# A hybrid decoder block in fp32 on one core: the first operands of the output projection prepared under the last merge unit, another order in the feed-forward's first unit, and the residual's reads behind a store

## The reference, cut to what matters

```python
merged = sigmoid(gate_a) * y_a + sigmoid(gate_b) * y_b     # y_a = o @ w_proj_a, y_b = zb @ w_proj_b
h = h + merged @ w_out                                     # 2048 x 2048
hn = rms_norm(h, norm_ffn_w)
h = h + (silu(hn @ w_gate) * (hn @ w_up)) @ w_down         # FFN width 5632
out = rms_norm(h, norm_final_w)[:, 16:]
```

## Time and profile before

| | us |
|---|---|
| median of 3 runs (2781.43 to 2783.2) | 2781.86 |
| the profiled execution | 2782.89 |
| its span, first to last instruction | 2781.1 |
| busy in the span: PE / DVE / ACT / POOL | 2694.5 / 1837.8 / 998.6 / 357.4 |
| mean granted TensorE clock (share of full) | 0.988 |

### The profile page before, as it was taken

How to read it: one execution, slowest core, us unless ns; L and a number is a source line. 1 busy time by engine, 2 the same in 40 slices (tenths; PEclk the granted TensorE clock), 3 DMA queues, 4 the chain that set the end, 5 groups by cost and what they waited for, 6 DMA issues and landing times.

```text
span 2781.1 us, 44509 instructions
## 1 busy us (share of the span) xinstructions
PE 2694.5 (97%) x17640; PEld 2451.1 (88%) x17640; DVE 1837.8 (66%) x1766; ACT 998.6 (36%) x1025; POOL 357.4 (13%) x356
## 2 busy tenths in 40 slices
PE   8999999999999999988979999999999998999997
PEld 7999988888889977867869999999999997788885
DVE  4444555555553234448888888888788887888886
ACT  4433322222222232213344444444444443333333
POOL 5000144444442500110030000000000000000000
PEclk9999999999999999999989999999999999999998
DMA  4333222222223324677434444544445449656661
GB/s 142 91 90 90 77 76 77 82 76 82 75 83 91 106 83 162 233 263 261 138 121 148 143 147 145 171 153 152 148 154 169 147 132 306 232 189 211 214 210 61
DMA packets 345652, 398.70 MB, mean 143 GB/s; under 512 B 11481, under 2 KB 300386, under 8 KB 344418
## 3 DMA queue, kind: packets, MB, share of 16 engines
q1 hardware_dynamic: 286514, 334.34, 37.5%
q10 hardware_dynamic: 59072, 63.44, 6.6%
HBM read 325.92 MB, written 71.83 MB: 143 GB/s over the span
## 4 chain that ended last, share of the span: by engine, by line
PE 92%; DVE 3%; issue 2%; DMA 1%; POOL 1%; ACT 1%; SPq 0%; DVEq 0%; ACTq 0%; POOLq 0%
PE psum L1869 33%; PE psum L2181 10%; PE psum L2180 10%; PE psum L2179 10%; PE psum L2156 6%; PE psum L2157 6%; PE psum L2158 6%; PE psum L2029 2%; PE psum L2024 1%; PE psum L1819 1%; PE psum L1847 1%; DMA w_raw<-in_w_proj_a 1%; PE psum L2008 1%; DVE hq L1657 1%; PE psum L2101 0%
## 5 line engine op out<-in xcount | busy, mean ns | idle before, releaser
L1869 PE MATMUL psum<-hn_lo,w_hi 128*128 128x264 f32 (+1 forms) x1600 | 453.5, 332 | 0.0
L1869 PE MATMUL psum<-hn_hi,w_lo 128*128 128x264 f32 (+1 forms) x1600 | 453.4, 332 | 0.0
L1869 PE MATMUL psum<-hn_hi,w_hi 128*128 128x264 f32 (+1 forms) x1600 | 452.8, 332 | 0.0
L1235 DVE TENSOR_TENSOR w_lo<-w_raw,w_hi 128x1024 fp32r<-128x1024 f32 x176 | 227.2, 1292 | 330.9 <-ACT w_hi L866 330.4
L866 ACT ACTIVATE w_hi<-w_raw 128x1024 fp32r<-128x1024 f32 x176 | 185.1, 1056 | 452.4 <-PE psum L1869 397.5
L1869 PEld LDWEIGHTS psum<-hn_hi,w_hi 128*128 128x128 f32 x1600 | 270.4, 189 | 23.0 <-issue 0.2
L1869 PEld LDWEIGHTS psum<-hn_lo,w_hi 128*128 128x128 f32 x1600 | 269.5, 188 | 23.9 <-issue 0.7
L1869 PEld LDWEIGHTS psum<-hn_hi,w_lo 128*128 128x128 f32 x1600 | 269.8, 189 | 23.2
L2156 PE MATMUL psum<-dn_hi,act_hl 128*128 128x512 f32 x616 | 244.6, 397 | 14.0 <-DVE hq L1657 12.9
L2157 PE MATMUL psum<-dn_lo,act_hl 128*128 128x512 f32 x616 | 244.0, 396 | 0.0
L2158 PE MATMUL psum<-dn_hi,act_hl 128*128 128x512 f32 x616 | 243.0, 395 | 0.0
(11 more groups left out here) (350 smaller groups left out, 6276.9 us busy)
## 6 DMA issues: line engine op xcount, KB each, us to landing
w_raw<-in_w_in SPq DMA_DIRECT2D x144, 512.0 KB, 3.6
ffn_raw<-in_w_ffn_gate SPq DMA_DIRECT2D x44, 1024.0 KB, 6.5
ffn_raw<-in_w_ffn_up SPq DMA_DIRECT2D x44, 1024.0 KB, 6.5
dn_raw<-in_w_ffn_down SPq DMA_DIRECT2D x40, 1024.0 KB, 7.2
act_hl<-act_dram SPq DMA_DIRECT2D x70, 512.0 KB, 9.0
act_dram<-comb_hi ACTq DMA_DIRECT2D x22, 896.0 KB, 4.2
act_dram<-comb_lo ACTq DMA_DIRECT2D x22, 896.0 KB, 6.3
out_raw<-in_w_out SPq DMA_DIRECT2D x16, 1024.0 KB, 10.0
```

The costliest lines, as they stand in the source:

```text
L1235: dve.tensor_tensor(wlo[s][:], raw[s][:], whi[s][:].bitcast(F32), ALU.subtract).then_inc(S["lo_ready"], 1)
L1869: ins = pe.matmul(o, lhs, r, start=kt == 0 and i == 0, stop=kt == 4 * n_chunks - 1 and i == 2)
```

## The change

It has four parts, of which the last leaves the order of work as it was.

1. *Last merge unit.* ScalarE makes the high parts of OUT's first three operands b11, b21 and t2 in the last merge unit, ahead of mg_hi. VectorE makes the sums t1, t3, the low part of b11, the sum t2 and the low part of b21 (a new function rows_begin) between the gate_a and the gate_b instructions of that unit, and the low part of t2 behind gate_b. rows_dve leaves them out.
2. *Residual's reads.* SP waits for the store of merge unit 6 before it issues the four reads of the residual's first half.
3. *The feed-forward's first unit.* ScalarE makes hi_2, hi_b and hi_c right behind hi_a, ahead of the pieces of s_hi; the rest of its first unit has an order of its own (first_unit_act). VectorE makes low_2 and low_b ahead of rows_read 6 and low_c behind it, copies the identity into the two diagonals of tiles 2 and 3 beforehand and multiplies them in place; the sum S2 is made in S4's buffer, low S2 comes ahead of the sum S4, and the low part of A22, two pieces on GpSimd before, is one VectorE instruction.
4. *Down projection.* rows_begin(DN) stands ahead of up_products, both ahead of rows_dve(DN).

```diff
             act_load(OUT, 0, "b21")
+            sp.wait_ge(S["comb_stored"], 32 * (N_MERGE - 1))
             h_load(OUT, 0, (H_11, H_12, H_22, H_21))
             sp.wait_ge(S["chunk_used"], G_OUT)
...
+            def merge_act(u, splits=True):
+                for c in range(4):
+                    if c == 3:
+                        if not splits:
+                            rows_split(OUT, 0, "b11")
+                            rows_split(OUT, 0, "b21")
+                            rows_split(OUT, 0, "t2")
+                        act.wait_ge(S["mg_sum"], 4 * u + 4)
...
+            def rows_begin(st):
 
                 rows_sum(st, 0, "t1")
                 rows_sum(st, 0, "t3")
+                rows_low(st, 0, "b11")
+                rows_sum(st, 0, "t2")
+                rows_low(st, 0, "b21")
+
+            def rows_dve(st, beside=lambda m, q: None):
+
                 for m in range(st.units()):
                     for q, what in enumerate(st.order(m)):
+                        if m == 0 and q < (3 if st is OUT else 2):
+                            continue
...
+            def merge_dve(u, splits=True):
...
+                    if c == 3:
+                        if not splits:
+                            rows_begin(OUT)
+                        for m in range(2):
...
+                                                     ALU.add, ALU.mult).then_inc(S["yb_gated"], 1)
+                        if not splits:
+                            rows_low(OUT, 0, "t2")
...
             split_a(0, 0)
+            split_2(0)
+            split_b(0)
+            split_c(0, 0)
             for n, (c, t, kh) in enumerate(A_PIECES[0:4]):
...
+            def first_unit_act():
+
+                evict_p1(0, 0)
+                s_high(S1, s_sum[S1][:], 1)
+                s_high(S2, s_sum[S4][:], 2)
+                s_high(S3, s_sum[S3][:], 3)
+                for c, t, kh in A_PIECES[4:6]:
+                    act.activation(s_piece(s_hi, c, t), y_piece(t, kh), ACT.Copy).then_inc(S["x_hi"], 1)
+                evict_u2(0, 0)
+                s_high(S4, s_sum[S4][:], 4)
+                evict_q5(0, 0)
+                split_a(0, 1)
+                split_2(1)
+                split_b(1)
...
             t_four(0, 0)
+            for t in range(2, TT):
+                dve.tensor_copy(diag[TT + 1 + t][:], ident[:]).then_inc(S["vectors_more"], 1)
...
             low_a(0, 0)
+            low_2(0)
+            low_b(0)
             rows_read(OUT, last, 6)
+            low_c(0, 0)
+            dve.wait_ge(S["vectors_more"], 4)
             for t in range(2, TT):
                 sum_of_h(t)
-                diagonal(TT + 1 + t)
+                dve.wait_ge(S["x_rms"], TT + 2 + t)
+                one = diag[TT + 1 + t][:]
+                dve.tensor_scalar(one, one, rms[:, TT + 1 + t:TT + 2 + t], None, ALU.mult).then_inc(S["x_diag"], 1)
...
+            s2_sum = s_sum[S4]
             dve.wait_ge(S["x_weighted"], 4 * (2 * TT + 1))
             dve.tensor_tensor(by_tile(s_sum[S1]), y_half(1, 0), y_half(1, 1), ALU.subtract).then_inc(S["s_sum"], 1)
             dve.wait_ge(S["s_sum"], 1)
-            dve.tensor_tensor(by_tile(s_sum[S2]), by_tile(s_sum[S1]), y_half(0, 0), ALU.subtract).then_inc(S["s_sum"], 1)
-            low_2(0)
+            dve.tensor_tensor(by_tile(s2_sum), by_tile(s_sum[S1]), y_half(0, 0), ALU.subtract).then_inc(S["s_sum"], 1)
             dve.tensor_tensor(by_tile(s_sum[S3]), y_half(0, 0), y_half(1, 0), ALU.subtract).then_inc(S["s_sum"], 1)
-            dve.wait_ge(S["s_sum"], 2)
-            dve.tensor_tensor(by_tile(s_sum[S4]), by_tile(s_sum[S2]), y_half(0, 1), ALU.add).then_inc(S["s_sum"], 1)
+            dve.wait_ge(S["s_sum"], 3)
+            s_low(S2, s2_sum[:], 6)
+            s_low(S1, s_sum[S1][:], 5)
+            c_11(0, 0)
+            dve.wait_ge(S["x_lo_v"], X0 // 2 + 1)
+            dve.tensor_tensor(by_tile(s_sum[S4]), by_tile(s2_sum), y_half(0, 1), ALU.add).then_inc(S["s_sum"], 1)
+            s_low(S3, s_sum[S3][:], 7)
             dve.wait_ge(S["s_sum"], 4)
-            s_low(S2, 6)
-            s_low(S1, 5)
+            s_low(S4, s_sum[S4][:], 10)
+            dve.wait_ge(S["x_hi"], X0 + 9)
+            dve.tensor_tensor(by_tile(s_lo[A22]), y_half(1, 1), by_tile(s_hi[A22]).bitcast(F32), ALU.subtract) \
+                .then_inc(S["x_lo_v"], 1)
...
-                low_pieces(4 * i, 4 + 2 * i)
+                low_pieces(4 * i, 4)
...
+            rows_begin(DN)
+            up_products(PAIRS - 1)
             rows_dve(DN, beside_down)
```

More of the change, by code:

```diff
@@ L1076, in rows_split @@
                     .then_inc(S["hi_ready"], 1)
+            def merge_act(u, splits=True):
[6 more added lines that the diff above has]
+                        act.wait_ge(S["mg_sum"], 4 * u + 4)
+                        after(act, "comb_stored", 32 * u)
+                        act.activation(mg_hi[:], mg[:, 0:7, :], ACT.Copy, scale=0.5).then_inc(S["merged_hi"], 1)
+                    if splits:
+                        split(G_MERGE + 4 * u + c + 4, c)
+                act.wait_ge(S["merged_hi"], u + 1)
+                act.wait_ge(S["merged_lo"], u + 1)
+                for hl, src in enumerate((mg_hi, mg_lo)):
+                    dst = mg_dram[hl, :, u] if isinstance(u, int) else \
+                        mg_dram[hl, :, bass.ds(u, 1)].rearrange("c o p t -> (c o) p t")
+                    act.dma_start(dst.rearrange("c p t -> p c t"), src[:].bitcast(F32)).then_inc(S["comb_stored"], 16)
+            with act.Fori(0, N_MERGE - 1) as u:
+                merge_act(u)
+            merge_act(N_MERGE - 1, False)
             squared = [0]
@@ L1177, in beside @@
                         comb_high(j - 1)
-                unit_act(j, 0, False, beside)
+                if first:
+                    first_unit_act()
+                else:
+                    unit_act(j, 0, False, beside)
                 if not first:
@@ new lines, in rows_begin @@
+            def rows_begin(st):
+                rows_sum(st, 0, "t1")
+                rows_sum(st, 0, "t3")
+                rows_low(st, 0, "b11")
+                rows_sum(st, 0, "t2")
+                rows_low(st, 0, "b21")
+            def rows_dve(st, beside=lambda m, q: None):
+                for m in range(st.units()):
+                    for q, what in enumerate(st.order(m)):
+                        if m == 0 and q < (3 if st is OUT else 2):
+                            continue
+                        if m > 0 and q == 0:
+                            rows_sum(st, m, "t1")
+                            rows_sum(st, m, "t3")
+                        if what == "b21":
+                            rows_sum(st, m, "t2")
+                        x = 7 * m + q
+                        if x >= 3:
+                            rows_read(st, (x - 3) // 7, (x - 3) % 7)
+                        rows_low(st, m, what)
+                        if q == 3:
+                            rows_sum(st, m, "t4")
+                        beside(m, q)
@@ L1660, in rows_dve @@
-            def rows_dve(st, beside=lambda m, q: None):
-                rows_sum(st, 0, "t1")
-                rows_sum(st, 0, "t3")
-                for m in range(st.units()):
-                    for q, what in enumerate(st.order(m)):
-                        if m > 0 and q == 0:
-                            rows_sum(st, m, "t1")
-                            rows_sum(st, m, "t3")
-                        if what == "b21":
-                            rows_sum(st, m, "t2")
-                        x = 7 * m + q
-                        if x >= 3:
-                            rows_read(st, (x - 3) // 7, (x - 3) % 7)
-                        rows_low(st, m, what)
-                        if q == 3:
-                            rows_sum(st, m, "t4")
-                        beside(m, q)
@@ L1784, in beside_down @@
             def beside_down(m, q):
-                if m == 0 and q == 1:
-                    up_products(PAIRS - 1)
                 if m == 0 and q == 3:
                     comb_low(PAIRS - 1)
+            rows_begin(DN)
+            up_products(PAIRS - 1)
             rows_dve(DN, beside_down)
```

185 lines of the change are left out of this document (86 added, 99 removed).

## The result

The kernel got slower: 2790.33 us (2790.03 to 2792.76, 8 runs) against 2781.97 (2779.9 to 2783.98, 8 runs), a ratio of 1.0031 with a 95% interval of 1.0022 to 1.004, or 8.4 us. The forecast was 2782.2 with a range of 2775 to 2790. It was wrong, and the true time lies just above the range. The profiled execution took 2790.37 us, its span 2788.2 (before 2781.1), so 7.1 us are to be found in it.

The account below looks back on a forecast made before the run. TensorE bounds the kernel, so only its waits pay: output part -3.0 us, feed-forward +3.3, down projection 0, together +0.3 on the median 2781.86, giving 2782.2 us; range 2775 to 2790.

Parts of the forecast that it names:

- The start of OUT, the hold, t2.: Output projection: first product starts at the merge's end, store in at 1243, t2 at 1253.5 after a 2.1 us wait.
- So the second unit starts at 1295.0.: Output projection: block (1,3) lands at 1289.4, low b11 ends 5.6 us after sum t3 starts; 5.5 us won, 3.0 after clock loss.
- The passes' exclusion and the turn.: Feed-forward's first unit: VectorE and GpSimd passes alternate, so the turn of tiles 2 and 3 shifts 7.5 us, to 1436.9.
- the proportional reading: Feed-forward's first unit: both engines slow down in proportion instead of excluding each other; turn shift 6.0 us, not 7.5.
- From W on: Feed-forward, from the first sum: S2 product at W + 9.3, weights issued W + 14, next unit W + 28.6; 2.2 us lost.
- Their landing: Feed-forward: second unit's weights, two issues 0.5 us apart and 6.5 us to landing, are in at W + 21.
- Each costs 0 to 2.5 us; I take 1.1 for both together.: Feed-forward: fallen clock after TensorE's waits ahead of A22 and the turn, 1.1 us in total.
- The down projection: Down projection: rows_begin ahead of up_products keeps the same passes in the same order; 0 us.
- The slower rival: Feed-forward turn after 1438 with low clock, 7.2 lost; output block at 1291.5 or later; 2788.1 and more, chance 0.22.

Follow-up runs that it names:

- b1_read_first: Kernel before plus early output operands and hold, with the read of the first unit's t3 product ahead of both second-unit sums; 2780.2 us, ratio 0.9989.
- c2: b2_queue plus only A22's low part as one VectorE instruction behind low S4, instead of GpSimd pieces; 2770.5 us, ratio 0.996.
- b3_sums_first: a2_ffn_only with rows_read 6, sums and diagonals directly behind low_a, and low_2, low_b, low_c behind them; 2788.98 us, ratio 1.002.
- b4_c22_first: a2_ffn_only with C_22 of the first unit ahead of low_a of the next; 2787.44 us, ratio 1.0015.
- b2_queue: b1_read_first without the hold, blocks (1,0), (1,1) queued ahead of the last store's wait, residual's second half behind block (1,3); 2771.82 us, ratio 0.9958.
- a2_ffn_only: Kernel before with only the feed-forward's first unit in the new order; 2788.72 us, ratio 1.0023.
- d1_c22_a22: c2 with C_11 and low_c first, then C_22, A22's low part and the next unit's low_a; 2768.58 us, ratio 0.9948.

## Why the prediction was wrong

Point by point, by its own steps.

- *The start of OUT, the hold, t2.* Right in kind, too early in size. The hold brought the store in 4.1 us behind the merge's end, not 2.7, and t2 started 15.6 behind it, not 13.2, so its wait was 4.4 us and not 2.1. Behind it the clock was low: the first matmul took 0.77 us, and the product 1261.97 - 1253.83 = 8.1 us instead of 5.5, a loss that the sum didn't have. It cost nothing here, as the next stall was tied to the block.
- *"So the second unit starts at 1295.0."* **This step failed.** The block came 2.1 us later behind the merge's end than forecast, which is a matter of size. The step itself asked which operand of the second unit was behind the block, and left out that the first unit's t4 product was behind it too: it writes over the bank that the read empties, and the read stood in VectorE's order behind sum t3. The same rule had been applied to t2. Instead of 5.5 us won, a product of 5.5 us was moved behind the stall, and the 3.0 us of parts 1 and 2 are gone. From the block to the end of that product it took 1300.37 - 1289.44 = 10.9 us; the step had 5.6 and 2.5 for the clock. b1_read_first, where only this read is moved, gives 3 us against before: the block is as late there, but low b11 follows sum t3 at once, and the product behind the stall loses 1.7 us to the clock, not 2.5.
- *The passes' exclusion and the turn.* Right in kind: the read at 1429.85 (forecast 1430.7), the turn at 1435.67 (1436.9), its shift against the last output product 6.1 us (7.5). The shift alone would suit the proportional reading (6.0) better, the single passes don't: lo_b took 4.42 us, its own 2.28 and most of another one, and lo_c, begun at 1430.98, ended at 1434.32, a pass's step of 2.2 behind the end of GpSimd's four (1417.71 + 14.46 = 1432.17), as if it had done nothing until then. The missing 1.4 us are earlier starts, GpSimd's by 0.4 and the end of lo_a by 0.5 among them. The rule of the Trainium skill (SBUF — State Buffer, Who interferes with whom), by which the second engine waits for the first one's whole instruction, agrees with these passes. And c2, with GpSimd's A22 pieces gone, won 4.2 us ahead of S2.
- *From W on* (W is the start of the first sum, 1445.47). The S2 product at W + 9.3 was met exactly (1454.77 - 1445.47). The issue of the weights was at W + 13.9 (14). **Their landing was mis-sized**: hi_a began 9.6 us behind the issue, not 7.0, so C_22 was at W + 27.7 where the step had W + 25.2. The 6.5 us in the earlier trace rows is a median over 44 transfers. And part 3 itself put other transfers beside these: SP asks for the next pair's gate weights once lo_c of the first unit is made, which is now early, so 2 MB more were queued from 1460.76 on, 1.4 us behind (before 16). More on this stands in the last section.
- *"Each costs 0 to 2.5 us; I take 1.1 for both together."* **Mis-sized.** The clock fell at both. From the turn's start to W it took 9.8 us, before 8.2; A22's product took 1478.39 - 1473.59 = 4.8 us, not 2.9. That is 3.5 us.
- *The down projection:* neutral, as said. From its first matmul to the end of the span it is 464.4 us, before 464.3.

The sum, redone: parts 1 and 2 gave +1.9 and not -3.0 (+2.1 the late block, +2.8 the t4 product and the read behind it); part 3 gave +6.8 and not +3.3 (-1.4 the turn, +2.4 the clock, +2.5 the weights). Together that is +8.7 where the forecast had +0.3, and the ratio says 8.6.

The slower rival named nearly the right time, 2788.1 and more, by half of its mechanism: the low clock over the turn and at A22 was there, but the turn was not later than 1438 and the block not later than 1291.5. The rest was the read, which was in no rival. The sign of what is missed this way is known beforehand, since a wait that was overlooked only adds; the range's upper end, taken from the terms that were written down, had no room for it.

## What to carry to other kernels

When a stall moves to a late transfer, go through the order of every engine that waits for it, and list each instruction behind that wait with its consumers, those of the unit before too: one read of 1.2 us behind a sum that it didn't need cost as much as the change won. Passes are hidden only if they stand in a wait of their own engine; moved from behind an event to ahead of it, they delay it by their length, and every event that hangs on it, an issue of the next weights among them. When one cover is taken away, look at the queue of transfers first: three lines of its order, together with the hold taken out, were worth 8 us here, and the operands made early, with the read in its place, 3 without them. A pass made early also frees its buffer early, and the load that waits for that buffer then runs beside the one that is needed. And when an upstream stage ends at another time in each run, compare from its end, or an agreement of absolute times says nothing.

## What was not expected of the hardware

- The clock is lost behind short waits too. Behind the 3.5 us ahead of A11 the first matmul of 256 columns took 0.55 us where 0.28 is usual, and the whole product ran slow: 5.3 us from start to end (1427.93 to 1433.2), 2.8 before (1425.91 to 1428.72). That one was under cover, as the turn waited for its diagonals anyway; those at the turn and at A22 were not. The length of the wait alone does not decide it: 2.5 us ahead of A11 in b3_sums_first were followed by a first matmul of 0.36 us and a product at full pace, 2.0 us ahead of the next unit in b4_c22_first by one of 0.55, and 1.8 us ahead of OUT's second unit in b2_queue by a granted clock of 0.50 to 0.52 over 1288 to 1291 us.
- The second unit's weights let hi_a begin 9.6 us behind their first issue (9.4 in a2_ffn_only, 9.6 in b4_c22_first). In all three the next pair's gate weights were issued 1.4 us behind them, and the DMA moved 337 to 380 GB/s from 1461 to 1472 us, twice the 2 MB of the pair. In c2_before_ffn_a22 and d1_c22_a22, where those gate weights were issued only 14 to 16 us later, it was 8.3 and 8.4. So sharing the queue costs about 1.2 us; this is read across kernels that differ in more than that. The other 1.3 us against the forecast's 7.0 most likely lie in the median: hi_a needs the later of two transfers. ScalarE's row in c2:

```profile
1444.79 1.92 ACT L1113 ACTIVATE hi_a<-ffn_raw 128x2048 fp32r<-128x2048 f32 x1 [0.91 <-DMA ffn_raw<-in_w_ffn_up]
```

- What stands behind the stores hardly moves against the merge's end: block (1,3) was in 50.5 to 51.6 us behind it in the five profiles with part 1 and the old order of the queue, with the hold or without. The forecast's 49.1 was the landing of before and 0.6 us, and 2.1 us short.
